# The first chunk's products take x by channels, without its row factors

## The reference

```python
def rms_norm(x, gain):
    xf = x.astype(jnp.float32)
    y = xf * lax.rsqrt(jnp.mean(xf * xf, axis=-1, keepdims=True) + EPS)
    return (y * gain.astype(jnp.float32)).astype(x.dtype)

        n1 = rms_norm(h, norm1_gain[l])
        proj = n1 @ w_in[l]
        u, v, q, f, i, g = jnp.split(proj, split_at, axis=-1)
        ...
        b_out = hgrn2_mixer(q, f, i, g, lb_all[l], hgrn_out_gain[l])
```

## Time and profile before

| | us |
|---|---|
| median of 3 runs | 1473.09 (1472.93 to 1476.5) |
| the profiled execution | 1476.15 |
| its span in the trace | 1474.4 |
| first product with weights (L777) | 15.87 |
| first product of chunk 1 | 29.90 |
| last product of chunk 5 ends | 86.55 |

### The profile page before, as it was taken

One profiled execution on the slowest core, in us unless ns is written; L12 is line 12 of the kernel. 1 busy time (PEld: TensorE's weight loads), 2 busy tenths in 40 slices (PEclk: granted clock), 3 DMA queues, 4 the chain that ended last, 5 costly groups with the idle time before them and its releaser, 6 DMA issues.

```text
span 1474.4 us, 15358 instructions
## 1 busy us (share of the span) xinstructions
PE 1285.1 (87%) x5264; PEld 679.7 (46%) x5264; DVE 717.1 (49%) x1553; ACT 535.0 (36%) x1281; POOL 322.7 (22%) x310
## 2 busy tenths in 40 slices
PE   6998899999898989899999699999877867887776
PEld 6874533333333333488898444454423323333322
DVE  4173310010001000387877775666677766666744
ACT  4442211111111111456663354434543444444433
POOL 6810000000000000000001333344433434443330
PEclk9998999999999999999999999999988999988899
DMA  9563799999999999974335989999999999999995
GB/s 354 187 242 132 295 387 426 428 430 433 424 431 425 429 430 433 335 300 172 115 129 213 419 329 411 419 412 416 419 421 419 421 421 419 420 420 419 420 420 242
DMA packets 63179, 531.39 MB, mean 360 GB/s; under 512 B 12040, under 2 KB 14344, under 8 KB 16520
## 3 DMA queue, kind: packets, MB, share of 16 engines
q0 software_dynamic: 36864, 268.45, 44.2%
q1 hardware_dynamic: 26248, 262.09, 43.6%
HBM read 529.47 MB, written 1.97 MB: 360 GB/s over the span
## 4 chain that ended last, share of the span: by engine, by line
PE 61%; DMA 22%; DVE 11%; ACT 4%; issue 2%; SPq 0%; POOL 0%; POOLq 0%; ACTq 0%; DVEq 0%
PE bank L1922 18%; DMA held<-in_uv,row_of 13%; PE bank L1654 12%; PE bank L777 7%; DMA ring_pair<-in_w_gate_up 6%; PE bank L1584 6%; PE bank L1883 4%; PE bank L1678 3%; PE bank L778 2%; DMA up_b<-in_w_gate_up 2%; DVE held L2533 2%; PE bank L1489 2%; PE bank L1867 1%; PE bank L1801 1%; DVE ti L2449 1%
## 5 line engine op out<-in xcount | busy, mean ns | idle before, releaser
L1922 PE MATMUL bank<-held,diags 128*128 128x512 f32 x1024 | 488.1, 631 | 118.1 <-ACT diags L1365 117.8
L2533 DVE SCALAR_TENSOR_TENSOR held<-held,bank 128x1024 f32<-128x1024 f32 x256 | 306.2, 1219 | 192.9 <-DMA held<-in_uv,row_of 192.9
L1922 PEld LDWEIGHTS bank<-held,diags 128*128 128x128 f32 x1024 | 199.4, 201 | 402.4 <-issue 215.1
L1043 POOL DMA_INDIRECT held<-in_uv,row_of x256 | 242.3, 947 | 619.7 <-PE bank L1922 387.5
L2201 DVE TENSOR_TENSOR hid<-bank,hid 64x512 f32<-64x512 f32 x32 | 22.2, 695 | 401.5 <-ACT hid L1182 401.5
L1654 PE MATMUL bank<-ring_pair,x_blk 128*64 128x512 f32 x704 | 163.2, 618 | 14.3 <-DMA ring_pair<-in_w_gate_up 12.8
L1360 ACT ACTIVATE gelus<-dots 128x1 f32<-128x1 f32 x256 | 51.0, 199 | 227.6 <-DVE held L2533 226.8
L1365 ACT ACTIVATE diags<-const,hidden 128x128 f32<-128x128 f32 x256 | 103.0, 402 | 54.2 <-PE bank L1922 47.6
L1182 ACT ACTIVATE hid<-bank 64x512 f32<-64x512 f32 x32 | 18.9, 590 | 285.4 <-PE bank L1654 285.4
L1584 PE MATMUL bank<-ring,hT 128*64 128x512 f32 x512 | 115.5, 592 | 1.2 <-ACT hT L1186 1.2
L1021 POOL COPY x_blk<-xs 128x512 f32 x32 | 20.0, 627 | 420.9 <-PE bank L1654 377.6
(11 more groups left out here) (378 smaller groups left out, 1468.5 us busy)
## 6 DMA issues: line engine op xcount, KB each, us to landing
ring_pair<-in_w_gate_up SPq DMA_DIRECT2D x22, 4096.0 KB, 29.9
ring<-in_w_down SPq DMA_DIRECT2D x32, 2048.0 KB, 21.0
ring<-in_w_in SPq DMA_DIRECT2D x14, 2048.0 KB, 11.9
gate_a<-in_w_gate_up SPq DMA_DIRECT2D x9, 2048.0 KB, 26.2
up_a<-in_w_gate_up SPq DMA_DIRECT2D x9, 1024.0 KB, 28.2
up_b<-in_w_gate_up SPq DMA_DIRECT2D x9, 1024.0 KB, 30.1
ring<-in_w_out SPq DMA_DIRECT2D x4, 2048.0 KB, 7.5
ring<-in_w_q SPq DMA_DIRECT2D x4, 2048.0 KB, 7.5
```

Of the source, the lines that this page charges most:

```text
L1043: pool.indirect_dma_start(held[b][:, :], None, dram["uv"], bass.IndirectOffsetOnAxis(ap=row_of[:, i:i + 1], axis=0)).then_inc(row_full[b], 16)
L1922: last = pe.matmul(bank[SUM_BANK[t] + half][:, :], diags[i % DIAGS][:, :], held[i % ROWS_HELD][:, D + half * 512:D + (half + 1) * 512], st ...
L2533: dve.scalar_tensor_tensor(held[b][:, 0:D], held[b][:, 0:D], 1.0, two_banks[X_BANKS[t]][:, :], ALU.mult, ALU.mult, accum_out=dots[:, i:i + ...
```

## The change

The host passes x a second time as `xT`, laid out with channels on partitions. It is loaded in two halves into `x_cols`, between the two halves of weight chunk 0; the load of x by tokens into `h` moves behind the load of chunk 4. ScalarE makes `raw1_hi` and VectorE `raw1_lo` from `x_cols` and the gain, and chunk 0 (f) is multiplied with these, so its result lacks the row factor. GpSimd squares `x_cols` into `x_sq` (two operations); after the first half of chunk 0 TensorE multiplies a matrix of ones with it (8 products of 128x256), which gives each token's sum of squares in every partition. VectorE, ScalarE and VectorE make `rs_row` of it (mean, root, reciprocal, each 128x256). Then VectorE multiplies `x_cols` by gain and `rs_row` (8 operations), ScalarE copies to `nT_hi1` (8), VectorE takes `nT_lo` (8), and chunks 1 to 5 use these. VectorE multiplies the f banks by `rs_row` ahead of the sigmoid (2). TensorE runs 24 products of ones with ones at its start. The 16 transposes, the token-wise statistics and `xhat` of this stage go. The order of chunk 0's lead products becomes all with hi, then all with lo. The lead and rest of chunk 0's first half are both VectorE's now, and ScalarE's copy of chunk 1's first half moves ahead of the root.

```diff
+WARM_PRODUCTS = 24
...
+            if i == 0:
+                for x, ready in ((x_hi, raw1_act), (x_lo, raw1_dve)):
+                    pe.wait_ge(ready, 2 * half + 2)
+                    for dst, by_channel, tile, ends in outs:
...
-            sp.dma_start(h[:, :, :], dram["x"].rearrange("(t p) d -> p t d", p=P)).then_inc(x_in, 16)
...
+            sp.dma_start(ring[slot_of(0)][:, 0:piece], w_first[:, 0:piece]).then_inc(bias_in, 16)
+            sp.dma_start(param[:, :], dram["param"]).then_inc(keys_in, 16)
+            sp.dma_start(cols[:, 0:x_half], dram["xT"][:, 0:x_half]).then_inc(cols_part[0], 16)
+            sp.dma_start(cols[:, x_half:], dram["xT"][:, x_half:]).then_inc(cols_part[1], 16)
+            sp.dma_start(ring[slot_of(0)][:, piece:], w_first[:, piece:]).then_inc(ring_full[slot_of(0)], 16)
             sp.dma_start(const[:, 0:P], dram["const"][:, 0:P]).then_inc(const_in, 16)
-            sp.dma_start(param[:, :], dram["param"]).then_inc(const_in, 16)
-            for n in range(2):
-                load(n, w_in[IN1_ORDER[n]])
+            load(1, w_in[IN1_ORDER[1]])
...
-            for n in range(2, 6):
+            for n in range(2, 5):
                 load(n, w_in[IN1_ORDER[n]])
+            sp.dma_start(h[:, :, :], dram["x"].rearrange("(t p) d -> p t d", p=P)).then_inc(x_in, 16)
+            load(5, w_in[IN1_ORDER[5]])
...
+            for half in range(2):
+                pool.wait_ge(cols_part[half], 16)
+                view = slice(4 * half, 4 * half + 4)
+                pool.tensor_tensor(x_sq[:, view, :], x_cols[:, view, :], x_cols[:, view, :], ALU.mult).then_inc(stat_sum, 1)
+
             for i in range(SPLIT_IN2):
                 for half in range(2):
+                    if i == 0 and half == 0:
+                        pool.wait_ge(half_rest, 1)
+                        continue
                     pool_half(pool, i, half)
...
-            act_stats(act, 0)
-            act.wait_ge(const_in, 32)
-            act_nT_lead(act, 0, "gain1", nT_hi1)
+            act.wait_ge(keys_in, 16)
+            for b in range(4):
+                act.wait_ge(cols_part[b // 2], 16)
+                for k in (2 * b, 2 * b + 1):
+                    last = act.activation(raw1_hi[:, k, :], x_cols[:, k, :], ACT.Copy, scale=pr("gain1", k))
+                last.then_inc(raw1_act, 1)
             act.wait_ge(half_hi, 1)
             act_half(act, 0, 1)
+            act_half(act, 1, 0)
+            act.wait_ge(stat_mean, 1)
+            act.activation(rs_row[:, :], rs_row[:, :], ACT.Sqrt).then_inc(stat_root, 1)
+            for b in range(4):
+                act.wait_ge(xhat_ready, b // 2 + 1)
+                for k in (2 * b, 2 * b + 1):
+                    last = act.activation(nT_hi1[:, k, :], x_cols[:, k, :], ACT.Copy)
+                last.then_inc(nT_act, 1)
...
-            pe.wait_ge(const_in, 32)
-            pe_turn(pe, 0, xhat)
-            wait_nT_split(pe, 0)
+            pe.wait_ge(x_summed, 1)
+            for i in range(WARM_PRODUCTS):
+                pe.matmul(bank[3][:, 0:P], ones1[:, :], ones1[:, :], start=True, stop=True)
...
+                    if i == 0 and half == 0:
+                        pe.wait_ge(stat_sum, NT)
+                        for k in range(KD):
+                            last = pe.matmul(bank[0][:, 0:T], ones1[:, :], x_sq[:, k, :], start=(k == 0), stop=(k == KD - 1))
+                        last.then_inc(x_summed, 1)
+                if i == 0:
+                    pe.wait_ge(const_in, 16)
+                    wait_nT_split(pe, 0)
...
-            dve_stats(dve, link, 0)
-            dve_xhat(dve)
-            ring_wait(dve, HALVES[0][0][0])
+            dve.memset(ones1[:, :], 1.0).then_inc(x_summed, 1)
+            dve.wait_ge(bias_in, 16)
             dve.tensor_copy(half_lead(0, 0), half_in(ring, 0, 0)).then_inc(half_hi, 1)
-            dve.wait_ge(const_in, 32)
+            dve.wait_ge(keys_in, 16)
+
+            def raw_low(half):
+                for b in (2 * half, 2 * half + 1):
+                    dve.wait_ge(raw1_act, b + 1)
+                    for k in (2 * b, 2 * b + 1):
+                        last = dve.scalar_tensor_tensor(raw1_lo[:, k, :], x_cols[:, k, :], pr("gain1", k),
+                                                        raw1_hi[:, k, :].bitcast(F32), ALU.mult, ALU.subtract)
+                    last.then_inc(raw1_dve, 1)
+
+            raw_low(0)
+            dve_half(dve, 0, 0)
+            raw_low(1)
             dve.tensor_tensor(lbd[:, :], prs("lb0"), prs("lb1"), ALU.subtract).then_inc(lb_diff, 1)
             dve.tensor_tensor(gain_both[:, :], prs("gain12"), prs("gainf"), ALU.mult)
-            dve_nT_rest(dve, 0, "gain1", nT_hi1)
+
+            dve.wait_ge(x_summed, 2)
+            dve.tensor_scalar(rs_row[:, :], bank[0][:, 0:T], 1.0 / D, EPS, ALU.mult, ALU.add).then_inc(stat_mean, 1)
+            dve.wait_ge(stat_root, 1)
+            link(dve.reciprocal(rs_row[:, :], rs_row[:, :]))
+            for k in range(KD):
+                last = dve.scalar_tensor_tensor(x_cols[:, k, :], x_cols[:, k, :], pr("gain1", k), rs_row[:, :], ALU.mult, ALU.mult)
+                if k % 4 == 3:
+                    last.then_inc(xhat_ready, 1)
+            for b in range(4):
+                dve.wait_ge(nT_act, b + 1)
+                for k in (2 * b, 2 * b + 1):
+                    last = dve.tensor_tensor(nT_lo[:, k, :], x_cols[:, k, :], nT_hi1[:, k, :].bitcast(F32), ALU.subtract)
+                last.then_inc(nT_dve, 1)
+            for use in range(2):
+                dve.wait_ge(proj_done, use + 1)
+                dve.tensor_tensor(hF[:, 2 * use:2 * use + 2, :], bank[IN1_BANK[use]][:, :].rearrange("p (a t) -> p a t", a=2),
+                                  spread(rs_row[:, :].unsqueeze(1), [P, 2, T]), ALU.mult).then_inc(f_scaled, 1)
...
+        "xT": by_partition(g["x"].transpose(0, 2, 1))[0],
```

More of the change, by code:

```diff
@@ L572, in build @@
         gained = sem("gained")
+        x_summed = gained
+        X_SUMS = 2
         row_turned = sem("row_turned")
@@ L770, in pe_half @@
             lead_in = half_lead(i, half)
-            x_hi = raw_hi if raw else nT_hi1 if i < SPLIT_IN2 else nT_hi
-            x_lo = raw_lo if raw else nT_lo
+            x_hi = raw1_hi if i == 0 else raw_hi if raw else nT_hi1 if i < SPLIT_IN2 else nT_hi
+            x_lo = raw1_lo if i == 0 else raw_lo if raw else nT_lo
             def product(dst, by_channel, tile, w, x, k, start, stop):
@@ L781, in pe_half @@
             begins = True
-            for dst, by_channel, tile, ends in outs:
-                for x in (x_hi, x_lo):
-                    for k in range(4):
-                        start = begins and half == 0 and x is x_hi and k == 0
-                        last = product(dst, by_channel, tile, lead_in, x, k, start, False)
-                begins = ends
+            if i == 0:
+                for x, ready in ((x_hi, raw1_act), (x_lo, raw1_dve)):
+                    pe.wait_ge(ready, 2 * half + 2)
+                    for dst, by_channel, tile, ends in outs:
+                        for k in range(4):
+                            start = begins and half == 0 and x is x_hi and k == 0
+                            last = product(dst, by_channel, tile, lead_in, x, k, start, False)
+                        begins = ends
+            else:
+                for dst, by_channel, tile, ends in outs:
+                    for x in (x_hi, x_lo):
+                        for k in range(4):
+                            start = begins and half == 0 and x is x_hi and k == 0
+                            last = product(dst, by_channel, tile, lead_in, x, k, start, False)
+                    begins = ends
             last.then_inc(half_hi_used, 1)
@@ L1060, in _ @@
                     for half in range(2):
[L1061 to L1062 removed]
+                        if use or half:
+                            act_half(act, use // 2 + 1, half)
                 half = use % 2
[L1064 to L1065 removed]
+                view = dst[:, 2 * half:2 * half + 2, :].rearrange("p a t -> p (a t)")
+                if use < 2:
+                    act.wait_ge(f_scaled, use + 1)
+                    act.activation(view, view, ACT.Sigmoid).then_inc(proj_act, 1)
+                else:
+                    act.wait_ge(proj_done, use + 1)
+                    act.activation(view, bank[IN1_BANK[use]][:, :], ACT.Sigmoid).then_inc(proj_act, 1)
             for half in range(2):
@@ L1858, in _ @@
             for part in range(2):
-                pe.wait_ge(merged_lo, 2 * (part + 1))
+                pe.wait_ge(merged_lo, RAW_TURNS + 2 * (part + 1))
                 for half in range(2):
```

40 lines of the change are left out of this document (25 added, 15 removed).

## The result

| | kernel before | changed kernel |
|---|---|---|
| median of the runs, us | 1473.09 (1472.33 to 1476.5, 7 runs) | 1480.08 (1478.82 to 1481.56, 7 runs) |
| ratio | | 1.0046, 95% interval [1.0034, 1.0057] |
| profiled execution, us (span) | 1476.15 (1474.4) | 1481.25 (1479.2) |
| first product with weights, us | 15.87 | 10.83 |
| chunk 1 starts, us | 29.90 | 33.09 |

A forecast was written before the change was run, and what follows sets the result against it. The start chain up to chunk 1 (29.90 us) was taken as the bound, TensorE never idle behind it. Chunk 1 later by 4.4 plus 2.3 for the clock gave +6.7 on the median 1473.1: 1479.8 us, range 1471.0 to 1483.0.

The forecast's parts named there:

- the forecast's: Near 21 us GpSimd gets the port ahead of VectorE's tiny operations, keeps it to 25.5; chunk 1 at 34.3; chance 0.54.
- Landings: Loads at the start: x at 5.9, xT at 7.2 and 8.5, chunk 1 near 16.2, w_sT at 20.4 us.
- the first rival: Slips through: `lbd` and `gain_both` precede GpSimd's request, only scaling waits to 25.5; chunk 1 at 31.2, 1476.7 us; chance 0.16.
- The low splits: VectorE's low STTs of chunk 0's second half: second waits for GpSimd, ends at 20.5; fourth asked for at 20.8 us.
- The sums of squares: TensorE's 8 ones products: 1.7 us, double at low clock; x_summed at 19 to 23.5 us, before 25.5, costing nothing.
- The table load: ScalarE makes raw1_hi from 7.2 us, products with hi from 9.0; the root's table counted as loaded before.
- The row factor: Behind the sums: mean 0.48, root 0.45, reciprocal 1.8 us, ending at 28.5; eight scaling STTs at 0.41 each.
- Chunk 1 and the clock: Chunk 1 at 34.3, 4.4 us late; TensorE's clock falls in the idle gap, 2.3 us more, bounds 1.5 and 3.4.
- From the trace to the median: The trace's 1476.15 lies 3.06 us above the median; the difference +6.7 is put on the median 1473.1, giving 1479.8.
- No blocking: Rival: no alternation, or subtractions do not block STTs; chunk 1 at 27.5, -1.0 us in all, 1472.1; chance 0.18.
- All goes well: Rival: no blocking, reciprocal at 0.48, no clock fall; chunk 1 at 26.2, about -4.6 us, 1468.5; chance 0.06.
- Worse: Rival: fourth low STT late and GpSimd's next subtraction gets between the STTs, another 4.6 us; +11, 1484.5; chance 0.06.

The follow-up runs named there:

- second trace of before: The kernel before, unchanged, traced and timed once more; median 1472.77 us, ratio 0.9991, traced end 1472.12 us.
- its second trace: The changed kernel, unchanged, traced and timed once more beside the kernel before; median 1480.06 us, ratio 1.0047.
- VectorE first at the port: Changed kernel with GpSimd's subtractions of chunk 0's second half held until VectorE has put out its four low splits; 1479.87 us, ratio 1.0039.
- early table load: Changed kernel with one small ScalarE copy ahead of its wait for x, so the table load comes before the landing; 1479.36 us, ratio 1.0040.
- GpSimd-later kernel: Changed kernel with GpSimd's subtraction for chunk 1's first half held back until nT_lo is complete; 1474.41 us, ratio 1.0017.
- reordered kernel: Changed kernel with VectorE's four splits first, early table load, sums of squares and root earlier, row factor and scaled x in PSUM; 1470.59 us, ratio 0.9972.
- order-only kernel: The kernel with all five edits to the changed kernel, but row factor and scaled x put back into SBUF; 1477.38 us, ratio 1.0032.

## Why the prediction was right, step by step

The total was right and the main mechanism was the one forecast: an exclusive port, at which VectorE and GpSimd take turns. The path through it was not the forecast's, and several terms were off.

**Landings.** w_sT was put at "4.67 + 15.7 = 20.4 as now". That step failed. SP issues one after the other, and the change adds two issues ahead of w_sT: it went out at 5.93 and landed at 22.1. Of the 1.7 us, 1.26 are its later place in the queue, and the rest is a longer way, 16.1 us from issue to landing for the 15.7 of the earlier trace rows. The way is not a constant either: 16.3 in the second trace of before, and 14.9 to 16.8 in the ten traces of the changed kernel and its variants, which all issue the load at 5.68 to 5.93 and have it at 20.6 to 22.6. So the order near 21 us is partly the execution's own. With w_sT at 22.1, `lbd`, `gain_both` and the mean slipped through at 20.93 to 21.5, so the mechanism of the first rival came (chance 0.16), not the forecast's (0.54).

**Why the rival's price was too low.** It had the scaling wait to 25.5 and chunk 1 at 31.2, with w_sT at "21, say", which with the memset would already give 26.0. The wait lasts as long as GpSimd's subtraction, and that starts when w_sT has landed. In the changed kernel, its second trace, the one with VectorE first at the port and the one with the early table load, GpSimd's subtraction ends at 27.10, 27.42, 27.55 and 27.22, and chunk 1 starts at 33.09, 33.41, 33.54 and 33.21: 5.99 us later each time. That is the eight operations (one of them ending 0.28 after GpSimd, the other seven in 2.77), the last of nT_lo to 32.84, and 0.25 to TensorE. So chunk 1 waits for a 256 KB load that TensorE does not use before 100 us, by way of a memset of 0.31 us. This is also why neither the first meeting nor the table load moved it. No run moved the memset or the load by itself, and an earlier landing is no gain of its own: in the kernel without ones products w_sT was there 1.5 us earlier, the subtraction got in ahead of `lbd`, and chunk 1 came 1.4 later.

**The low splits.** Predicted: the second of four waits for GpSimd to 20.2 and the last is asked for at 20.8; measured: one of 4.793 us, and all four from 15.02 to 21.00. Right, and covered by TensorE, as the experiment shows.

**The sums of squares.** Priced at 1.7 us, measured 3.62. The row that I used lists 48 entries, which I took for 48 products; a plain float32 product appears as two (8 products of the code are x16 here), so the price was half. The 24 leading products are x48 and took 8.0 us, not 5.5. (GpSimd's squares were cheaper than put: 3.74 us for both, not 4.6.) It cost nothing in the changed kernel, since the mean waited for VectorE to 21.08 anyway; the sums ended at 20.8. With the port free it is the next limit, as the 4.00 us of waiting above show.

**The table load.** 1.28 us of ScalarE between the landing of x and the first split (7.69 to 8.97) was not in the sum; the table loads that the prediction names are those ahead of the root and of lb. With x landed 0.5 us later than put, it accounts for the first products at 10.83 instead of 9.0. Not on the path either, as the experiment shows.

**The row factor.** Mean 0.41 (0.48), root 0.42 and 0.02 (0.45), reciprocal 1.75 (1.8, taken from the slope of the earlier trace rows); eight scaling operations undisturbed 3.25 (3.3). The estimate of 2.1 to 2.3 us from the Trainium skill's repeat count (VectorE: DVE Perf Modes, "First, the fixed hardware budget"), which took one cycle for each repeat, is not what this trace shows; the slope of the rows was the better guide.

**Chunk 1 and the clock.** 34.3 was predicted, 33.09 and 33.41 measured, 34.51 where the forecast's order came. The fall of the clock came as predicted; it cost 1.77, inside the bounds 1.5 and 3.4, below the 2.3 taken. "TensorE's clock here costs nothing", said of chunk 0, held for this kernel; with the port free in time it does not (0.9 us in the GpSimd-later kernel). Sum: 3.19 + 1.77 = 4.96 in place of 4.4 + 2.3 = 6.7.

**From the trace to the median.** The profiled execution of before stands 3.06 us above its median; I carried the difference over unchanged. The difference of the two medians, 7.0, is 2.0 more than that of the two first traces and equal to that against the second trace of before. The predicted 6.7 is so close to 7.0 partly by luck: the terms added up to more than this pair of traces shows, and the pair shows less than the medians.

**The other rivals.** No blocking is excluded (3.620 and 4.793 us). "All goes well" is nearly what the reordered kernel reaches: chunk 1 at 25.85 (26.2 there) and 3.1 us off the median of the runs beside it (4.6 there). "Worse", a further subtraction among the scaling operations, did not come in the changed kernel, where GpSimd's next one starts at 34.91, when ScalarE has made its lead; in the order-only kernel two (16.41 and 21.88) meet the scaling.

## What to carry to other kernels

Where VectorE's operations with two SBUF inputs stand beside GpSimd's long ones, look for the one instance with a maximum far above the median, and first try to give it one input in PSUM: here that turned 9.37 us into 3.23. Expect to need the order as well: either alone left the kernel no faster than before. Follow the neighbour's release as well as your own chain: GpSimd's start, and so chunk 1, hung on a load that nobody needed yet, behind two more issues in a DMA queue and with a landing that varies by 2 us between executions. And take a second trace of the kernel before, when the difference sought is of the size of its own scatter.

## What the runs showed of the hardware that I had not expected

- Turn taking is strict even for the smallest operation: `lbd`, 128x4, took 4.54 us because GpSimd's request came 0.09 us earlier; in the changed kernel, with GpSimd's request at 22.5, it took 0.15.
- An idle TensorE of 3.18 us kept its clock in one kernel, one of 3.46 us lost it in another, and one of 6.55 us lost it. Even the same program differed: the clock of before rose at 21.5 in one trace and 19.3 in the other, and one of its later low stretches lasted 6.8 us in the one and 3.4 in the other. The executions of before differ by some 6 us (1471.47 to 1477.79 in one set of 20), more than any gain at the front tried here; only the median of ten runs shows the reordered kernel's 3.1.
- From 1 to 20 elements the reciprocal rises 6.3 ns an element; the whole 128x256 one took 1.75 us, (1753 - 158) / 255 = 6.3 ns an element again.
